# Choosing experts from 112 pairs of ranks instead of 256, with threshold masks in two bytes

## The reference: what is computed

```python
def peer_chunk(xc, w_query, sub_keys, peer_u, peer_v):
    C = xc.shape[0]
    q = (xc @ w_query).reshape(C, PEER_HEADS, 2, D_KEY_HALF)
    s = jnp.einsum('chpd,hpnd->chpn', q.astype(jnp.float32), sub_keys.astype(jnp.float32))
    s1, i1 = lax.top_k(s[:, :, 0], PEER_TOPK)
    s2, i2 = lax.top_k(s[:, :, 1], PEER_TOPK)
    cand_s = (s1[..., :, None] + s2[..., None, :]).reshape(C, PEER_HEADS, PEER_TOPK * PEER_TOPK)
    cand_i = (i1[..., :, None] * N_KEYS + i2[..., None, :]).reshape(C, PEER_HEADS, PEER_TOPK * PEER_TOPK)
    top_s, top_pos = lax.top_k(cand_s, PEER_TOPK)
    idx = jnp.take_along_axis(cand_i, top_pos, axis=-1)
    g = jax.nn.softmax(top_s, axis=-1)
    u = peer_u[idx]
    a = jax.nn.gelu(jnp.einsum('cd,chkd->chk', xc, u).astype(jnp.float32), approximate=False)
    v = peer_v[idx]
    return jnp.einsum('chk,chkd->cd', (g * a).astype(v.dtype), v).astype(xc.dtype)
```

## Time and profile before

| | us |
|---|---|
| median of 3 runs | 3658.21 |
| the runs | 3639.86 to 3660.15 |
| span of the profiled execution | 3659.0 |
| VectorE busy in it | 2704.0 |
| TensorE busy | 3082.9 |
| GpSimd busy | 2336.6 |
| ScalarE busy | 921.9 |
| moved by DMA | 1259.50 MB, 344 GB/s |

### The profile page before, as it was taken

One profiled execution on the slowest core, in us unless ns is written; L12 is line 12 of the kernel. 1 busy time (PEld: TensorE's weight loads), 2 busy tenths in 40 slices (PEclk: granted clock), 3 DMA queues, 4 the chain that ended last, 5 costly groups with the idle time before them and its releaser, 6 DMA issues.

```text
span 3659.0 us, 32490 instructions
## 1 busy us (share of the span) xinstructions
PE 3082.9 (84%) x8982; PEld 1564.7 (43%) x8982; DVE 2704.0 (74%) x6074; ACT 921.9 (25%) x2252; POOL 2336.6 (64%) x1940
## 2 busy tenths in 40 slices
PE   7897697899986987777987986458999998889998
PEld 4664343467553433333433431134543445544333
DVE  2218877787679988878998899977975579955555
ACT  2112232422223321153222121134410015510000
POOL 0006543677556766878776667786877668877775
PEclk9898897778998998887998998779999999899999
DMA  6359986899999999998999999998999999899999
GB/s 152 105 173 364 356 276 199 303 376 376 346 357 375 361 378 312 333 345 316 402 388 396 403 355 370 347 358 320 337 409 409 409 408 371 311 377 409 409 409 369
DMA packets 425721, 1259.50 MB, mean 344 GB/s; under 512 B 61000, under 2 KB 106728, under 8 KB 425531
## 3 DMA queue, kind: packets, MB, share of 16 engines
q0 software_dynamic: 276480, 1006.76, 72.6%
q1 hardware_dynamic: 141125, 244.91, 19.8%
q10 hardware_dynamic: 7936, 5.77, 0.5%
HBM read 1229.04 MB, written 28.25 MB: 344 GB/s over the span
## 4 chain that ended last, share of the span: by engine, by line
PE 35%; DVE 15%; DMA 14%; POOL 13%; issue 10%; SPq 2%; ACT 2%; another core or an unknown queue 1%; ACTq 0%; DVEq 0%; POOLq 0%
DMA vbuf<-in_peer_v_dram,idx 9%; PE pY L1667 8%; POOL ubuf L942 8%; PE pb L1538 6%; POOL vbuf L954 5%; DVE ubuf L2327 4%; PE pb L1640 4%; PE pb L1292 3%; PE pb L1556 3%; DVE acc L2348 2%; PE pb L1627 2%; DMA ubuf<-in_peer_u_dram,idx 1%; PE pb L1584 1%; DMA R<-c_scratch 1%; PE pb L1511 1%
## 5 line engine op out<-in xcount | busy, mean ns | idle before, releaser
L942 POOL DMA_INDIRECT ubuf<-in_peer_u_dram,idx x1088 | 1367.0, 1256 | 917.9 <-DVE dots L2327 320.2
L2327 DVE CUSTOM_DVE_ANT_0 ubuf<-ubuf,hnf 128x1024 f32<-128x1024 f32 x1088 | 1314.4, 1220 | 331.6 <-DMA ubuf<-in_peer_u_dram,idx 288.7
L1667 PE MATMUL pY<-vbuf,dg 128*128 128x512 f32 (+1 forms) x1956 | 1039.1, 662 | 242.5 <-DMA vbuf<-in_peer_v_dram,idx 139.8
L954 POOL DMA_INDIRECT vbuf<-in_peer_v_dram,idx x832 | 966.7, 1162 | 390.5 <-issue 230.8
L1667 PEld LDWEIGHTS pY<-vbuf,dg 128*128 128x128 f32 (+1 forms) x1956 | 366.9, 200 | 740.0 <-issue 508.5
L2348 DVE SCALAR_TENSOR_TENSOR acc<-vbuf,gw,acc 128x1024 f32<-128x1024 f32 x343 | 439.9, 1282 | 57.4 <-DMA vbuf<-in_peer_v_dram,idx 48.4
L1640 PE MATMUL pb<-R 128*128 128x512 f32 x1024 | 460.3, 593 | 1.2 <-issue 0.7
L1538 PE MATMUL pb<-R 128*128 128x256 f32 (+2 forms) x1152 | 361.7, 475 | 8.9 <-DMA R<-in_w_in_dram 4.4
L1929 ACT ACTIVATE gel<-dots 128x4 f32<-128x4 f32 x272 | 55.5, 204 | 1076.3 <-DVE dots L2327 863.5
L1640 PEld LDWEIGHTS pb<-R 128*128 128x128 f32 x1024 | 194.6, 191 | 245.2 <-issue 243.9
L1538 PEld LDWEIGHTS pb<-R 128*128 128x128 f32 x1152 | 221.6, 193 | 145.7 <-issue 93.0
(11 more groups left out here) (252 smaller groups left out, 2717.7 us busy)
## 6 DMA issues: line engine op xcount, KB each, us to landing
R<-in_peer_v_dram SPq DMA_DIRECT2D x128, 512.0 KB
R<-in_w_in_dram SPq DMA_DIRECT2D x12, 2048.0 KB
R<-in_w_in_dram SPq DMA_DIRECT2D x24, 1024.0 KB
R<-in_w_query_dram SPq DMA_DIRECT2D x24, 1024.0 KB
ubuf<-in_peer_u_dram,idx POOLq DMA_INDIRECT x1088
vbuf<-in_peer_v_dram,idx POOLq DMA_INDIRECT x832
R<-in_w_out_dram SPq DMA_DIRECT2D x12, 1024.0 KB
R<-in_x_prompt_dram SPq DMA_DIRECT2D x16, 512.0 KB, 8.8
```

Of the source, the lines that this page charges most:

```text
L942: pool.indirect_dma_start(out=ubuf[:, n % RING, :], out_offset=None, in_=peer_u[0], in_offset=bass.IndirectOffsetOnAxis(ap=idx[:, t % NI, ...
L954: pool.indirect_dma_start(out=vbuf[:, v % RING, :], out_offset=None, in_=peer_v[0], in_offset=bass.IndirectOffsetOnAxis(ap=idx[:, t % NI, ...
L1667: ins = pe.matmul(pY[0:rows, half, :], dg[:, CPE[m] % RDG, 0:rows], vbuf[:, v % RING, half * 512:(half + 1) * 512], start=first, stop=(t ! ...
L2327: dve.tensor_tensor_reduce(ubuf[:, n % RING, :], ubuf[:, n % RING, :], hnf[:, par, :], 1.0, 0.0, ALU.mult, ALU.add, dots[:, q % 2, n % GRP ...
```

## The change

The row ranks and column ranks are sorted, so a pair (i, j) counted from 0 has at least (i+1)(j+1) - 1 better or equal ones before it. Of rows 4 to 15, columns 4 to 15 can't be among the 16 best. `top_b` sums the first 4 rows with all 16 columns (64 places) and the other 12 rows with the first 4 columns (48 places), and searches these 112.

A place is turned into its row by 16 thresholds `firsts` (0, 16, 32, 48, 64, 68, ... 108): the mask place >= threshold is multiplied by the differences of successive row keys and summed, which gives the key of the row. The column rank comes from the low bits of the place (all four below 64, two from there on), and is compared with 0 to 15 as before. `i16` has a column of zeros in front for the differences. Masks and key numbers are bfloat16, two bytes each; whole numbers of this size are exact in it. The constants of `spread` are written out as numbers. The buffer `R` is 32 elements shorter.

Left out of the diff below: four waits for `c_sel` that count to 18 instead of 16, on TensorE (two), ScalarE and VectorE.

```diff
--- before.py
+++ after.py
@@ -44,6 +44,9 @@
     NK = sub_keys.shape[3]
     TOPK = 16
     NPICK = PH * TOPK
+    WIDE, THIN = 4, 4
+    NCAND = WIDE * TOPK + (TOPK - WIDE) * THIN
+    assert all((i + 1) * (j + 1) > TOPK for i in range(WIDE, TOPK) for j in range(THIN, TOPK))
     NPC = PH * 2
     HALF = NPICK // 2
     SCALE = float(DH) ** -0.5
@@ -159,6 +162,7 @@
 
 
     PASSES = [(3, 5)]
+    PASS_AT = [708, 1082]
     DENSE = [t for pair in PASSES for t in pair]
     assert S not in DENSE and NPICK == P and D == 1024
     GATHERED = [t for t in range(NT + 1) if t not in DENSE]
@@ -545,19 +549,20 @@
             DUE.setdefault(n0 + int((n1 - n0) * run / total), []).append(slot)
             run += wt
 
+    GROUP_AT = [(0, 50), (50, 280), (281, 600)]
+    CHOOSE_AT = {1: (52, 108), 3: (282, 364), 4: (410, 492), 6: (602, 684), 7: (730, 812), 8: (858, 940)}
     ALONE = []
     for g in range(GN):
         slots, ready = lay_out(g)
         if g == 0:
             ALONE = slots[:ready]
-            spread(slots[ready:], 0, 50)
+            spread(slots[ready:], 0, GROUP_AT[0][1])
         else:
-            spread(slots, START[FIRST[g - 1]] + (50 if g == 1 else 25), START[FIRST[g]] + 24)
-    for t in range(NT + 1):
-        if t not in FIRST:
-            spread(choose(t), START[t - 1] + (52 if t == 1 else 26), ENDS[t - 1] - 20)
-    for ps, pair in enumerate(PASSES):
-        spread(dense(ps), ENDS[pair[1]] + 4, NPK - 6 if ps + 1 == len(PASSES) else ENDS[PASSES[ps + 1][1]] + 4)
+            spread(slots, *GROUP_AT[g])
+    for t in CHOOSE_AT:
+        spread(choose(t), *CHOOSE_AT[t])
+    for ps in range(len(PASSES)):
+        spread(dense(ps), PASS_AT[ps], PASS_AT[ps + 1])
 
     every = ALONE + [slot for n in sorted(DUE) for slot in DUE[n]]
     SN = {args: k for k, args in enumerate([x[1] for slot in every for x in slot if x[0] == "s_mm"])}
@@ -678,16 +683,19 @@
         s_sb = sb("s_sb", [P, 2, 2, NK])
 
         eq = sb("eq", [P, 4, TOPK, TOPK])
-        cand, cand_rest = (eq[:, k].rearrange("p a b -> p (a b)") for k in range(2))
+        cand, cand_rest = (eq[:, k].rearrange("p a b -> p (a b)")[:, 0:NCAND] for k in range(2))
         s_rest = eq[:, 2].rearrange("p a b -> p (a b)").rearrange("p (c n) -> p c n", c=2)
-        i16 = sb("i16", [P, 4, TOPK], U32)
-        i16f = sb("i16f", [P, 4, TOPK])
+        i16 = sb("i16", [P, 4, TOPK + 1], U32)
+        i16b = sb("i16b", [P, 4, TOPK], BF16)
+        firsts = sb("firsts", [P, TOPK])
+        idx_f = sb("idx_f", [P, 2, TOPK])
+        eqb = eq[:, 0:2].rearrange("p c a b -> p (c a b)").bitcast(BF16).rearrange(
+            "p (c a b) -> p c a b", c=4, a=TOPK)
         part_i = sb("part_i", [P, 4, TOPK], U32)
         part_f = sb("part_f", [P, 4, TOPK])
         half_i = part_f
         top_s = sb("top_s", [P, 2, TOPK])
         top_p = sb("top_p", [P, 2, TOPK], U32)
-        idx_f = i16f[:, 0:2]
         dif = sb("dif", [P, 2, TOPK])
         gsum = sb("gsum", [P, 2])
         ginv = sb("ginv", [P, 2])
@@ -705,9 +713,9 @@
         gel = sb("gel", [P, 2, GRP])
 
 
-        R = sb("R", [P, 22624])
+        R = sb("R", [P, 22592])
         R0, R1, R2 = R[:, 0:4096], R[:, 4096:8192], R[:, 8192:10240]
-        R3, RW, R4 = R[:, 10240:12320], R[:, 12320:20512], R[:, 20512:22624]
+        R3, RW, R4 = R[:, 10240:12320], R[:, 12320:20512], R[:, 20512:22592]
 
         def xnT(g):
             return R0[:, 0:KD * N_[g]].rearrange("p (c t) -> p c t", c=KD)
@@ -811,7 +819,7 @@
                 for k in range(OHR)]
         DT0 = DO0 + OHR * OHN
         dT = R[:, DT0:DT0 + 6 * P].rearrange("p (j x t) -> p j x t", j=2, x=3)
-        assert DT0 + 6 * P <= 22624
+        assert DT0 + 6 * P <= 22592
 
         ab_f = [R[:, DO0 + j * OHN:DO0 + j * OHN + 2 * P].rearrange("p (x k) -> p x k", x=2) for j in range(2)]
         ab_i = [R[:, DO0 + j * OHN + 2 * P:DO0 + j * OHN + 4 * P].bitcast(U32).rearrange("p (x k) -> p x k", x=2)
@@ -928,6 +936,10 @@
                           allow_small_or_imprecise_dtypes=True).then_inc(c_sel, 1)
                 pool.iota(iota[:], pattern=[[1, NK]], base=0, channel_multiplier=0,
                           allow_small_or_imprecise_dtypes=True).then_inc(c_sel, 1)
+                pool.iota(firsts[:, 0:WIDE], pattern=[[TOPK, WIDE]], base=0, channel_multiplier=0,
+                          allow_small_or_imprecise_dtypes=True).then_inc(c_sel, 1)
+                pool.iota(firsts[:, WIDE:], pattern=[[THIN, TOPK - WIDE]], base=WIDE * TOPK, channel_multiplier=0,
+                          allow_small_or_imprecise_dtypes=True).then_inc(c_sel, 1)
 
                 for n in range(NPK + LAG):
                     if n < NPK:
@@ -2258,23 +2270,26 @@
                         ins = dve.max(v16[R, n % 2, c, 0:8], s)
                     step(ins)
                     for c, s, rest in sides:
-                        dve.max_index(i16[R, 2 * (e % 2) + c, 0:8], v16[R, n % 2, c, 0:8], s)
+                        dve.max_index(i16[R, 2 * (e % 2) + c, 1:9], v16[R, n % 2, c, 0:8], s)
                         ins = dve.match_replace(rest, v16[R, n % 2, c, 0:8], s, LOWEST)
                     step(ins)
                     for c, s, rest in sides:
                         ins = dve.max(v16[R, n % 2, c, 8:16], rest)
                     step(ins)
                     for c, s, rest in sides:
-                        ins = dve.max_index(i16[R, 2 * (e % 2) + c, 8:16], v16[R, n % 2, c, 8:16], rest)
+                        ins = dve.max_index(i16[R, 2 * (e % 2) + c, 9:17], v16[R, n % 2, c, 8:16], rest)
                     ins.then_inc(s_u, 1)
 
                 def top_b(t, e):
 
                     n, rows = SN[t, e], rows_of(t)
                     R, k = slice(0, rows), e % 2
-                    step(dve.tensor_tensor(cand[R, :].rearrange("p (a b) -> p a b", a=TOPK),
-                                           v16[R, n % 2, 0, :].unsqueeze(2).to_broadcast([rows, TOPK, TOPK]),
-                                           v16[R, n % 2, 1, :].unsqueeze(1).to_broadcast([rows, TOPK, TOPK]), ALU.add))
+                    for c0, i0, i1, w in ((0, 0, WIDE, TOPK), (WIDE * TOPK, WIDE, TOPK, THIN)):
+                        shape = [rows, i1 - i0, w]
+                        ins = dve.tensor_tensor(cand[R, c0:c0 + (i1 - i0) * w].rearrange("p (a b) -> p a b", b=w),
+                                                v16[R, n % 2, 0, i0:i1].unsqueeze(2).to_broadcast(shape),
+                                                v16[R, n % 2, 1, 0:w].unsqueeze(1).to_broadcast(shape), ALU.add)
+                    step(ins)
                     step(dve.max(top_s[R, k, 0:8], cand[R, :]))
                     dve.max_index(top_p[R, k, 0:8], top_s[R, k, 0:8], cand[R, :])
                     step(dve.match_replace(cand_rest[R, :], top_s[R, k, 0:8], cand[R, :], LOWEST))
@@ -2284,18 +2299,25 @@
                 def fin_a(t, e, w):
 
                     rows, n = rows_of(t), SN[t, e]
-                    R, E, C, shape = slice(0, rows), slice(e % 2, e % 2 + w), slice(2 * (e % 2), 2 * (e % 2 + w)), [rows, 2 * w, TOPK, TOPK]
+                    R, E, C, shape = slice(0, rows), slice(e % 2, e % 2 + w), slice(2 * (e % 2), 2 * (e % 2 + w)), [rows, w, TOPK, TOPK]
+                    E2 = slice(2 + e % 2, 2 + e % 2 + w)
                     if n:
                         dve.wait_ge(ge_d, n)
                     dve.tensor_tensor(dif[R, E], top_s[R, E], top_s[R, E, 0:1].to_broadcast([rows, w, TOPK]), ALU.subtract
                                       ).then_inc(df_d, w)
-                    dve.tensor_scalar(part_i[R, C][:, 0::2, :], top_p[R, E], 4, None, ALU.logical_shift_right)
-                    dve.tensor_copy(i16f[R, C], i16[R, C])
-                    step(dve.tensor_scalar(part_i[R, C][:, 1::2, :], top_p[R, E], TOPK - 1, None, ALU.bitwise_and))
-                    step(dve.tensor_copy(part_f[R, C], part_i[R, C]))
-                    step(dve.tensor_tensor(eq[R, C], part_f[R, C].unsqueeze(3).to_broadcast(shape),
+                    dve.tensor_scalar(part_i[R, E], top_p[R, E], THIN - 1, None, ALU.bitwise_and)
+                    dve.tensor_tensor(i16b[R, C][:, 0::2, :], i16[R, C, 1:][:, 0::2, :], i16[R, C, :TOPK][:, 0::2, :], ALU.subtract)
+                    dve.tensor_copy(i16b[R, C][:, 1::2, :], i16[R, C, 1:][:, 1::2, :])
+                    step(dve.tensor_scalar(part_i[R, E2], top_p[R, E], TOPK - THIN, None, ALU.bitwise_and))
+                    dve.tensor_tensor(eqb[R, C][:, 0::2], top_p[R, E].unsqueeze(3).to_broadcast(shape),
+                                      firsts[R].unsqueeze(1).unsqueeze(1).to_broadcast(shape), ALU.is_ge)
+                    step(dve.scalar_tensor_tensor(part_f[R, E], top_p[R, E], float(WIDE * TOPK), part_i[R, E2], ALU.is_lt,
+                                                  ALU.mult))
+                    step(dve.tensor_tensor(part_f[R, E], part_f[R, E], part_i[R, E], ALU.add))
```

(13 more changed lines are left out.)

## The result

| | before | after |
|---|---|---|
| median of 17 runs, us | 3651.7 | 3628.2 |
| the runs, us | 3636.3 to 3668.3 | 3615.8 to 3652.7 |
| span of the profiled execution | 3659.0 | 3651.0 |
| VectorE busy in it | 2704.0 | 2642.0 |

The ratio of after to before is 0.9942, with a 95% interval of 0.9927 to 0.9957: 21 us, between 16 and 27 (the two medians lie 23.5 us apart). The forecast was 3639, 19.7 us less, in a range of 3610 to 3663, with "the same within 1%" at 0.81.

What follows compares the result with a forecast made beforehand. The bound differs by stage: VectorE from 275 to 405 and 1049 to 1180 us, DMA, then GpSimd later. Gains of 15.6 us before 2030 us and 4.1 after make 19.7, from 3659.0 to 3639, range 3610 to 3663.

Steps and rivals of the forecast that it cites:

- The price of the parts: VectorE work saved in all: 0.78 us per top_b, +0.35 per two-head fin_a, -0.1 per single one; 62 us.
- Rival D: In fin_a, the two-byte product isn't faster: gain 14 us, 3645; shares the forecast's chance of 0.53.
- Its place on the chain: Only part of VectorE's saving shortens the chain of waits: 31 of 72 heads counted on it, gain 19.7 us.
- The two stages that it named as shorter: Windows to 405 us and from 1049 to 1180 us, VectorE nearly full: shorter by about 4 and 5 us.
- before 2030 us: 15.6 us: Chain before 2030 us: 21 heads save 16.4, single fin_a cost 1.5, double ones give 0.7.
- Rival A: Heads on the chain have a second bound just behind, so the saving is hidden: gain 0 to 6 us; chance 0.22.
- The latter I halve, to 4.1: Chain after 2030 us: ten heads' 8.3 us halved, as DMA is full or GpSimd hardly waits for VectorE.
- The two heads before the first pick: Heads before 306.5 us, where the chain can't be followed, counted on it as they run on VectorE alike.
- The sum: Total gain on the chain, before and after 2030 us together: 19.7 us on a span of 3659.0.
- Rival C: GpSimd issues gathers more slowly beside dots than beside the choice: 23 us lost, 3663 to 3682; chance 0.08.
- Rival B: The saving counts beyond the chain, as shorter choices let GpSimd start earlier elsewhere: gain 30 to 62 us; chance 0.17.

Runs made afterwards that it cites:

- e5: Kernel before with top_b in tiles 0 to 3 cut to 64 places and 8 repeated picks, 50 us less VectorE: ratio 0.9955, -16 us.
- e9: Kernel before with the 112 pairs in top_b for tiles 0 to 3 alone, places split by the old rule: ratio 0.9979, -8 us.
- e10: Kernel before with the 112 pairs in top_b for tiles 4 to 8 alone, places split by the old rule: ratio 0.9999, 0 us.
- e6: Kernel before with top_b in tiles 4 to 8 cut to 64 places and 8 repeated picks, 60 us less VectorE: ratio 1.0004, +1 us.
- e11: The changed kernel, unchanged, run again against the kernel before, in the last four runs: ratio 0.9937, -23 us.
- e1: Kernel before with the 112 pairs alone in top_b, old masks and old splitting of places: ratio 0.9969, -11 us.
- e2: Changed kernel with all 256 pairs summed and searched, so the new masks alone, against the kernel before: ratio 0.9997, -1 us.
- e4: The changed kernel, unchanged, run again against the kernel before, in the first four runs: ratio 0.9965, -13 us.
- e3: Kernel before with its buffers moved to the changed kernel's addresses, nothing else: ratio 1.0002, +1 us.
- e8: Changed kernel with heads 2 to 7 of tiles 0, 2 and 5 finished in pairs, against the kernel before: ratio 0.9963, -13 us.
- e12: Changed kernel with heads 2 to 7 of tiles 0, 2 and 5 finished in pairs, run again against the kernel before: ratio 0.9948, -19 us.

## Why the prediction held, and where it did not

**The price of the parts** was right: 62 us of VectorE forecast and measured, 56 from the pairs and 6 from the masks. That it is so close is in part luck: three profiles of the change have 2639.5 to 2642.5 us. Inside it, `top_b` missed at MAX8, by 16 ns on 144 instructions or 2.3 us, and the 0.09 us that the sums save in each of 72 calls had been counted at nothing. MAX8 and FIND_INDEX8 over 64 elements, in e5's groups:

```profile
L2284 DVE MAX8 top_s<-eq 128x8 f32<-128x64 f32 x32 | 7.3, 228 | 1.1
...
L2285 DVE FIND_INDEX8 top_p<-top_s,eq 128x8 uint32<-128x64 f32 x32 | 7.0, 219 | 0.0
```

228 ns at 64, 278 at 112 and 428 at 256 lie on one line, 1.04 ns per element, as FIND_INDEX8 does (219, 269, 418). The row at 128 that I started from, 280 ns in `top_a`, lies 15 ns below it; why, no run tells. The product came out at the low ends of its bounds, 732 ns beside 690 and 425 beside 420. Rival D falls. The Trainium skill ("VectorE: DVE Perf Modes", section "The perf-mode tier table") had said both, double rate for the product and single rate for the reduction; the trace agrees, with 1225 against 732 ns and 1209 against 1209. From 512 to 1024 elements the product grows by 307 ns, where it grew by 533.

**Its place on the chain** was half right. The two stages that it named as shorter are shorter by what it said (4.5 and 5.2 us for 4 and 5). They hold 13 of the 21 heads that it counted before 2030 us (5 and 8, the first of the eight 1 us ahead of pick 251), and 13 x 0.78 is 10.1 us, beside the 9.7 measured. The term "before 2030 us: 15.6 us" was too large all the same: its pairs, 16.4 us, give 8 us (0 to 15) in e9. The step that failed is to count every head on the chain alike. Of the other eight no gain shows: four from 445 to 639 us lie in picks 40 to 128, which took 316.3 and 321.1 us with the long choice, 322.4 and 321.9 with the short one and 318.9 in e5; two lie in picks 286 to 384, where the two sets of profiles disagree (above), two before the first pick (below). A chain says which work was last, not by how much. The busy share of VectorE in the stage was the better guide: 97% and 94% in the two stages, 75% in picks 40 to 128 (and 91% in picks 286 to 384 in e10). Rival A, a second bound just behind, is thus true of most of the other heads, and of the stage of tile 2 beyond this dose: there e5 takes 11.5 us of VectorE's work away and gains 8.0, where picks 0 to 40 give 8.4 for 9.5.

**"The latter I halve, to 4.1"**: taken from the kernel before, it is nothing. e6 and e10 both give 0 after 1440 us. There, 690 of GpSimd's gathers of `peer_u` follow their predecessor at once and 35 wait for a dot; the chain of waits still named ten heads there. The row was the better witness. That GpSimd's pace, or full DMA engines, is why nothing was gained is argued from it: no run changes either.

**The two heads before the first pick** were counted in and gave nothing for the first. The timeline of the changed kernel has the reduction of head 0, a table load on ScalarE, and the reciprocal behind it:

```profile
283.78 0.69 DVE L2328 TENSOR_REDUCE part_f<-eq 128x32 f32<-128x512 bf16 x1
...
283.95 1.28 ACT L1906 ACT_TABLE_LOAD   x1
...
285.65 0.16 DVE L2334 RECIPROCAL ginv<-gsum 128x1 f32<-128x1 f32 x1 [1.19 <-ACT dif L1906]
```

The reciprocal waits 1.19 us for ScalarE's exponential (it was 0.44 us in the kernel before, and is 1.18 in e11 and 0.44 in e10, which has the long choice here). The exponential waits for the table load and, ahead of it, a copy of TensorE's result (L1883, at 283.33), so a shorter `top_b` only makes this wait longer.

**The sum** of 19.7 us is close to the 21 measured, and nearer than its terms, which is luck as far as the runs tell. Of 15.6 and 4.1 us, the pairs by tiles gave 8 and 0. The change itself gave 13 us beside e1 and e2 (whose 11 and 1 add up to that), 23 beside e9 and e10, and 21 (16 to 27) in the result. The intervals allow for the difference, and no run explains it. The profiles hold a hint: with the new masks, picks 704 to 960 took 819.2, 824.7 and 824.9 us (the given profile, e4, e2), without them 829.5, 827.0 and 826.7 (the given profile, e3, e1); on the other two chips 802.4, 810.1 and 804.8 (e11, e8, e12) with them, and 809.7 to 818.4 in the five runs without. That is some 5 and 9 us less in the mean, in two stages picked out afterwards from eleven, while e2 as a whole gave 1 us (between 11 less and 9 more). That the masks save time in the late tiles isn't shown; it stays open.

**Rival C**, slower gathers once the choice is short: the mean of GpSimd's gathers of `peer_u` went from 1256 to 1243 ns, and is 1251 in e3 and 1255 in e4. An issue that starts inside a dot does take longer, 1.41 us in the mean over both kinds of gather against 1.06 for the others in the kernel before, and 1.39 against 1.06 in the changed one; but 857 of them start inside one where 846 did. So there is something like its price, 0.35 us rather than 0.5, but the mean that was to grow did not. **Rival B** wanted a gain of 30 us or more, above the interval.

## What to carry to other kernels

Before costing a saving by the chain of waits, look at the busy share of the engine in each stage. Where it was busy nearly throughout (94 and 97%), what was taken from it shortened the stage by almost as much; where it was busy 75%, or where GpSimd's instructions mostly followed one another at once, savings were worth nothing that could be seen, even though the chain ran through them. Compare the lengths of stages, over more than one profile of each kind, before a chain is believed; a double dose shows in which stage a second bound lies. Parts measured one at a time can add up to the whole in one set of runs and not in another, when their intervals are as wide as the parts. A price by size is better drawn through rows of the same instruction in the same place than from one row of another place.

## What the runs showed of the hardware

The kernel before was 26 us slower on the chip of the first four runs than on those of the others (medians 3653.5, 3627.9 and 3627.3). The six profiles of the given pair and of e1 to e4 have waits that the profile attributes to no engine or queue of the program. Two of ScalarE's and one of GpSimd's in the changed kernel's first profile (total us, times, longest):

```profile
ACT R L1932 <- remote: 18.3, 3, 7.3
ACT R L1883 <- remote: 18.2, 2, 13.2
...
POOL vbuf L966 <- remote: 10.7, 5, 2.8
```

In total such waits were 87 us in 19 cases in this profile, 134 us in 28 in that of before, 92 in e2 and in e3, 125 in e4 and 133 in e1, so the changed kernel has neither more nor fewer of them. In the eight profiles of e5 to e12, on the other two chips, there are none. Many are hidden beside other work, and what they are can't be told from here, but they hit single steps by up to 14 us. Two of them are the 4.7 us lost in the first stage of the profile shown. That they are the difference between the chips isn't shown: the profiles give no sum of what they cost in time.
